# Second mixer of a hybrid trunk kernel: inverse kept in compact 32-column tiles, mean-free v, decays by ScalarE from running sums

## The reference

```python
r, k, v, xw, xa, xg = _split(h, RWKV_SPLITS)            # after the token shift mix
wlog = -softplus(-(w0 + tanh(xw) @ w2)) - 0.5
decay = exp(-exp(wlog))
a = sigmoid(a0 + xa @ a2);  g = sigmoid(xg) @ g2
kk = hd(k * k_k);  kk = kk / maximum(sqrt(sum(kk * kk)), 1e-12)
k = k * (1.0 + (a - 1.0) * k_a)
# scan over 512 tokens, 8 heads of 64:
sa = -einsum('bhvk,bhk->bhv', S, kk_t)
S = S * w_t + sa * (kk_t * a_t) + v_t * k_t;  y_t = S r_t
y = (y - mean(y)) * rsqrt(var(y) + eps)   # per head
y = (y * gn_g + gn_b + sum(r * k * r_k) * v) * g
# beside it, on the other 512 channels:
z = a_c * sigmoid(gate);  y_c = silu(layernorm(causal_conv31(z)))
```

## Time and profile before

| | |
|---|---|
| runs, median (lowest to highest) | 1389.52 us (1388.11 to 1390.04), 3 runs |
| profiled execution, own time | 1388.51 us |
| its span, mean granted clock | 1386.7 us, 0.967 |
| PE busy | 1279.2 us, 92%, 9060 instructions |
| PEld / DVE / ACT / POOL busy | 1038.0 / 682.2 / 421.6 / 518.6 us |
| w_hi*h_hi matmuls, L861, x696 | 283.7 us, 408 ns each |
| conv taps, L1807, x120 | 99.3 us, 827 ns each |
| w_lo, POOL, L501, x368 | 509.6 us, 1415 ns each |

### The profile page before, as it was taken

How to read it: one execution, slowest core, us unless ns; L and a number is a source line. 1 busy time by engine, 2 the same in 40 slices (tenths; PEclk the granted TensorE clock), 3 DMA queues, 4 the chain that set the end, 5 groups by cost and what they waited for, 6 DMA issues and landing times.

```text
span 1386.7 us, 21884 instructions
## 1 busy us (share of the span) xinstructions
PE 1279.2 (92%) x9060; PEld 1038.0 (75%) x9060; DVE 682.2 (49%) x992; ACT 421.6 (30%) x536; POOL 518.6 (37%) x374
## 2 busy tenths in 40 slices
PE   5999999999999999979798888787899999999997
PEld 4797978888888888856666656564688888888885
DVE  7435365551124444457758587675655511244334
ACT  4547333221122222253334324222432211222110
POOL 4341435554445555431121030110245544455541
PEclk9899999999999999989999999897999999999998
DMA  4331212222322223210011010000022232222221
GB/s 183 115 107 46 77 72 96 91 91 100 112 91 91 91 91 105 101 67 32 32 34 50 11 50 14 31 33 1 28 95 91 91 105 108 91 91 91 94 88 61
DMA packets 16808, 105.74 MB, mean 76 GB/s; under 512 B 1872, under 2 KB 2144, under 8 KB 4832
## 3 DMA queue, kind: packets, MB, share of 16 engines
q1 hardware_dynamic: 16304, 104.03, 21.1%
q10 hardware_dynamic: 432, 0.64, 0.1%
HBM read 102.57 MB, written 2.10 MB: 75 GB/s over the span
## 4 chain that ended last, share of the span: by engine, by line
issue 50%; PE 27%; POOL 21%; DVE 1%; DMA 0%; POOLq 0%; ACT 0%; SPq 0%; DVEq 0%
PE ps L861 23%; POOL w_lo L501 21%; PE ps L946 3%; PE ps L915 1%; DMA w_raw<-in_weights 0%; DVE x L1361 0%; PE ps L896 0%; POOL w_lo L490 0%; POOLq L495 0%; ACT w_hi L601 0%; POOLq L498 0%; SPq L454 0%; DVE xsq L1372 0%; DVE scaled L1431 0%; DVE x L1433 0%
## 5 line engine op out<-in xcount | busy, mean ns | idle before, releaser
L501 POOL TENSOR_TENSOR w_lo<-w_raw,w_hi 128x512 fp32r<-128x512 f32 x368 | 509.6, 1415 | 827.5 <-ACT w_hi L514 284.1
L861 PE MATMUL ps<-h_hi,w_hi 128*128 128x512 f32 x696 | 283.7, 408 | 11.6 <-POOL w_lo L490 11.6
L861 PE MATMUL ps<-h_lo,w_hi 128*128 128x512 f32 x696 | 275.0, 395 | 0.0
L861 PE MATMUL ps<-h_hi,w_lo 128*128 128x512 f32 x696 | 274.8, 395 | 0.0
L861 PEld LDWEIGHTS ps<-h_hi,w_hi 128*128 128x128 f32 x696 | 132.8, 191 | 51.3 <-issue 12.2
L589 ACT ACTIVATE w_hi<-w_raw 128x2048 fp32r<-128x2048 f32 x50 | 95.7, 1914 | 194.7 <-PE ps L861 143.4
L861 PEld LDWEIGHTS ps<-h_hi,w_lo 128*128 128x128 f32 x696 | 132.8, 191 | 28.7
L861 PEld LDWEIGHTS ps<-h_lo,w_hi 128*128 128x128 f32 x696 | 133.3, 192 | 25.9 <-issue 0.5
L861 PE MATMUL ps<-f_hi,w_lo 128*128 128x512 f32 x384 | 149.5, 389 | 0.0
L861 PE MATMUL ps<-f_hi,w_hi 128*128 128x512 f32 x384 | 149.5, 389 | 0.0
L861 PE MATMUL ps<-f_lo,w_hi 128*128 128x512 f32 x384 | 149.5, 389 | 0.0
(11 more groups left out here) (305 smaller groups left out, 1941.9 us busy)
## 6 DMA issues: line engine op xcount, KB each, us to landing
w_raw<-in_weights SPq DMA_DIRECT2D x93, 1024.0 KB, 4.9
outT<-x SPq DMA_DIRECT2D x8, 256.0 KB, 2.0
x<-in_xT SPq DMA_DIRECT2D x6, 256.0 KB, 7.3
masks_f<-in_masks SPq DMA_DIRECT2D x1, 768.0 KB, 10.6
x<-in_xT ACTq DMA_DIRECT2D x2, 256.0 KB, 5.6
w_raw<-in_weights SPq DMA_DIRECT2D x1, 512.0 KB, 6.4
low_w<-in_low_w SPq DMA_DIRECT2D x1, 512.0 KB, 11.3
sgu_ln<-in_sgu_ln SPq DMA_DIRECT2D x1, 512.0 KB, 3.6
```

The costliest lines, as they stand in the source:

```text
L501: piece = pool.tensor_tensor(w_lo[:, j, at], w_raw[:, j, at], w_hi[:, j, at].bitcast(f32), SUB)
L861: mm = pe.matmul(bank(gb(g) if isinstance(i, int) else g % 2), w, r, start=(k == 0 and m == 0), stop=(k == K - 1 and m == 2))
```

## The change

- **Inverse.** X and XT are block diagonal in 64 by 64 until the last level, so both are kept as `xc`, `xtc` (128 partitions, 8 matrices, 64 columns), as is TX (`txc`). `tx` and `dx` of levels 1 to 5 write 32 output columns each from 64 rows (`QUARTERS`), 32 columns moving: four matmuls per matrix for `tx`, four for the X update, and four for the XT update, which is now a step of its own, `dxt`, for all eight matrices at once (one VectorE copy instead of two). Level 6 makes only the off-diagonal quarter; ScalarE copies it into `XT`, and copies the two diagonals there (`xt_diag`). The banks alternate by level (`tx_bank`, `x_bank`).
- **Mean-free v.** v is brought to token rows by a matmul with `CEN` = identity - BLK/64 instead of a transpose, so that y comes out with no mean: the mean matmul, its subtraction and the step `yc` go. `ysq` is taken from the bank beside `y`. Gain and `gn_b` are folded into two VectorE steps; ScalarE's affine pass goes. `out_`, `conv_ln` and `taps` are split into single steps.
- **Decays.** The scan writes `cum`, with one zero column ahead of each chunk; ScalarE takes all exponentials from it, chunk by chunk, the chunk's middle as bias: 12 of 128 columns instead of 3 of 512, plus two scaled copies of 4 columns. Two VectorE subtractions go. `ak` moves from VectorE to ScalarE (`t_g`).
- **Order.** Slices are eighths (three matmuls), counts doubled. `evac_a`, `evac_q`, `evac_b` follow the last eighth of a tile at once, whatever comes next. `tok_tr` is a step of its own and waits for the X copies. `zpad` and `dsh` are double. A bank is free after `evac_a`. The tail is ordered anew.
- The mask table in DRAM shrinks from 1536 to 1025 columns.

The diff's core:

```diff
+QUARTERS = [(h, slice(a, a + 32)) for h in COLUMN_HALVES for a in (h.start, h.start + 32)]
...
             for lv in range(1, LEVELS):
-                ORDER1 += [("tx", c, lv, 0), ("tx", c, lv, 1)] + mid[lv] + fill(LEVEL_N[c][lv - 1])
-                ORDER1 += [("dx", c, lv, 0), ("dx", c, lv, 1)] + end[lv] + taps[lv]
+                ORDER1 += [("tx", c, lv, 0), ("tx", c, lv, 1)] + mid_[lv] + fill(LEVEL_N[c][lv - 1])
+                ORDER1 += [("xt_diag", c, 0), ("xt_diag", c, 1)] if lv == LEVELS - 1 else []
+                ORDER1 += [("dx", c, lv, 0), ("dx", c, lv, 1)]
+                if lv < LEVELS - 1:
+                    ORDER1 += [("dxt", c, lv)]
+                ORDER1 += end[lv] + taps[lv]
...
-            coming = [other[0] for other in ORDER1[at + 1:at + 4]]
-            if not scaled_yet or "dx" in coming:
+            if not scaled_yet:
                 continue
-            for t in begun:
-                order += [("evac_b", t), ("low", t)]
-            begun = []
             for t in held:
-                order += [("evac_a", t), ("evac_q", t)]
-                if t == held[-1] and t < 14 and coming[:1] in (["slice"], ["taps"]):
-                    begun += [t]
-                else:
-                    order += [("evac_b", t), ("low", t)]
+                order += [("evac_a", t), ("evac_q", t), ("evac_b", t)]
+                order += [("low", t)] if t < 2 else []
             held = []
...
+            def exps(c):
+                act.wait_ge(s("cum_done"), c + 1)
...
+                for dst, first, i, name, last in ((t_b, 0, 0, "ea_done", "at"), (t_c, 1, 1, "en_done", "kt"),
+                                                  (t_d, 1, 0, "ep_done", "rt")):
...
+                    for n in range(TT):
+                        one = act.activation(dst[:, n * P:n * P + P], cum[:, n, first:first + P], ACT.Exp,
+                                             bias=mid[:, i, n:n + 1], scale=(-EXP_HALF, EXP_HALF)[i])
...
+            def tok_tr(c, b):
+                pe.wait_ge(s("x_init"), 4 * c + 2)
...
+                    if b == 0:
+                        mm = pe.matmul(to, one, CEN[:, :], start=True, stop=True)
+                    else:
+                        mm = pe.transpose(to, one, IDENT)
...
                 for yy in range(4 * b, 4 * b + 4):
-                    for r in COLUMN_HALVES:
-                        mm = pe.matmul(as2(ps[r, 2 + b, 64 * (yy % 4):64 * (yy % 4) + 64], B), SC[:, yy, r],
-                                       half_of_one(X, yy, B, 0), start=True, stop=True)
+                    at = yy % 4
+                    if lv == LEVELS - 1:
+                        for to in (slice(64, 96), slice(96, 128)):
+                            mm = pe.matmul(ps[to, tx_bank(lv, b), 64 * at:64 * at + 64], SC[0:64, yy, to], xc[0:64, yy, :],
+                                           start=True, stop=True)
+                    else:
+                        for r, to in QUARTERS:
+                            mm = pe.matmul(as2(ps[to, tx_bank(lv, b), 32 * at:32 * at + 32], B), SC[r, yy, to],
+                                           side_of_one(xc, r, yy, B, 0), start=True, stop=True)
                 mm.then_inc(s("tx_mm"), 1)
...
+            def dxt(c, lv):
...
+                for yy in range(8):
+                    for r, to in QUARTERS:
+                        w = slice(to.start - r.start, to.stop - r.start)
+                        mm = pe.matmul(as2(ps[to, xt_bank(lv), 32 * yy:32 * yy + 32], B), txc[r, yy, w],
+                                       side_of_one(xtc, r, yy, B, 1), start=True, stop=True)
+                mm.then_inc(s("dxt_mm"), 1)
...
+            def xt_diag(c, h):
+                act.wait_ge(s("xt_upd"), 5 * c + 5)
...
+                r = COLUMN_HALVES[h]
+                act.activation(XT[r, :, r], xtc[r, :, :], ACT.Copy).then_inc(s("xt_diag"), 1)
```

More of the change, by code:

```diff
@@ L188, in build @@
             t_f = sb("t_f", [P, SEQ])
-            zpad = sb("zpad", [P, SEQ + TAPS - 1])
-            sgate = dsh
+            zpad = sb("zpad", [P, 2, SEQ + TAPS - 1])
             y = sb("y", [P, SEQ])
@@ L326, in build, with eighths @@
         TOK = {"v": (v_tok, 1), "sv": (sv, 5), "u": (u_tok, 7), "g": (g_tok, 9)}
-        def quarters(tiles):
-            return [("slice", t, q) for t in tiles for q in range(4)]
+        def eighths(tiles):
+            return [("slice", t, k) for t in tiles for k in range(KD)]
         def taps_in(c, counts):
             ends = [sum(counts[:i + 1]) for i in range(len(counts))]
[L336 to L341, removed]
-            + [("decay_v", 0, 2), ("kn", 0), ("kn_v", 0)] + quarters([14])[1:] + [("dyn", 0, 0)] \
-            + [("dyn", 0, 1)] + quarters([15])[:3] + [("bonus", 0), ("slice", 15, 3)]
+            return [[("tap", c, j) for j in range(e - n, e)] for n, e in zip(counts, ends)]
@@ new lines, in dyn @@
+        def dyn(c, names):
+            return [("dyn", c, name) for name in names]
+        ORDER1 = [("slice", t, k) for k in range(KD) for t in (0, 2)] + [("stat",)] \
+            + [("zero", i) for i in range(7)] + eighths([4]) + [("spread",)] + eighths([3])[:4] + [("zw", 0)] \
+            + eighths([3])[4:] + [("za", 0), ("ak", 0), ("scan", 0), ("ksq", 0), ("exps", 0)] \
+            + eighths([14])[:2] + [("ks", 0), ("ks_v", 0)] \
+            + [("dec", 0), ("kn", 0), ("kn_v", 0)] + eighths([14])[2:] + dyn(0, DYN[:3]) \
+            + dyn(0, DYN[3:]) + eighths([15])[:6] + [("bonus", 0)] + eighths([15])[6:]
@@ L351, in build @@
         for c in range(CT):
-            gaps = quarters(FILL[c])
+            gaps = eighths(FILL[c])
             def fill(n):
@@ L1827, in m @@
                 tt(M_LO1[k], M_SRC1[k], F(M_HI1[k]), SUB).then_inc(s("m_lo_done"), 1)
-            steps = {"stat": start, "spread": started, "evac_a": evac_a, "evac_b": evac_b, "decay_v": decay, "ks_v": ks, "kn_v": kn, "dyn": dyn, "bonus": bonus, "scores": scores,
-                     "dx": dx, "st": st, "post_v": post, "taps": taps, "conv_ln": conv_ln, "m": m}
+            steps = {"stat": lambda: norm(2), "zero": zero, "evac_a": evac_a, "evac_b": evac_b, "scan": scan, "dec": dec_,
+                     "ks_v": ks, "kn_v": kn, "dyn": dyn, "bonus": bonus, "scores": scores, "dx": dx, "dxt": dxt, "s": s_,
+                     "post_v": post, "tap": tap, "conv_sub": conv_sub, "conv_root": conv_root, "conv_scale": conv_scale, "m": m}
             for name, *a in ORDER1:
```

735 lines of the change are left out of this document (426 added, 309 removed).

## The result

The changed kernel is no faster: 1397.19 us, median of 15 runs (1388.41 to 1404.7), beside 1389.52 for the kernel before in as many. The ratio is 1.005, with a 95% interval of 1.0032 to 1.0068, so it is about 7 us slower, where 1370 was predicted with a range that ended at 1386. Runs 2 and 3 have one execution each in a slower state (1471.61 and 1499.3 us), which is left out of what is said of their time.

What follows compares the result with a forecast made beforehand. In the second mixer, TensorE with gaps bounds blocks 0 to 2, VectorE block 3. From 1388.5: -7.0 -8.9 -8.0 -5.5 -3.1 +2.5 +2.5 +1.0 +7.2 gives 1369.2, stated as 1370 us; range 1357 to 1386.

Steps and rivals of the forecast that it cites:

- The level matmuls: Levels 1 to 5 of the inverse: 192 records at 8 ns take 1.5 us a level, a gain of 1.3.
- the first step: Level matmul cadence, 1.5 us a level; wrong if a level's 192 records last over 2.5 us.
- Rival 3: tx, dx, dxt of levels 1 to 5: column tiles do not overlap, 29 ns a record, 1431 us; chance 0.06.
- The eager evacuations: Eager evac_b outside the first preparation leaves VectorE idle about 0.8 us a tile, mostly covered: 1.0 us slower.
- The first preparation: First block: `ak` and longer exponentials before the key norm's root, 1.6, and evac_b before dyn, 0.9: 2.5 us slower.
- Scores: v's real matmul with CEN and tok_tr waiting for the X copies: 2.5 us slower in sum.
- The clock: More TensorE idles of 3 to 4 us in blocks 0 to 2 lower the clock; four charged, 7.2 us.
- VectorE: VectorE's busy time falls by some 30 us through fewer copies, subtractions and updates.
- tail: Conv mean to output: mean matmul, its subtraction and ScalarE's affine pass leave the chain, 3.1 us gained.
- The sum of block 0: Block 0's six levels go from 43.0 to 36.0 us, 7.0 us gained.
- Second step's mark: TensorE's waits in 590 to 989 us: growth of more than 15 us would prove that step wrong.
- rival 2: Blocks 0 to 2: savings turn into waits through evacuations before copies and ScalarE's queue; 1384 us, chance 0.14.

Runs made afterwards that it cites:

- run 2: Changed kernel with level matmuls in 64 by 64 tiles, each issued twice: 1447.86 us, ratio 1.0449 to the kernel before.
- run 3: Kernel before with 1920 added small matmul records of 64 by 32 tiles in levels 1 to 5: 1482.31 us, ratio 1.0659.
- run 4: Changed kernel with dxt of levels 1 to 5 issued twice: 1433.98 us; with dxt for only four of eight matrices: 1380.59 us.
- run 1: Changed kernel with level matmuls in 64 by 64 tiles instead of 64 by 32: 1406.27 us, ratio 1.0098 to the kernel before.
- run 6: Old evacuation rule (none while dx is among the next three steps): on the changed kernel 1385.68 us, on its 64 by 64 form 1397.16 us.
- run 7: Changed kernel with block 0's twelve exponentials moved behind the key norm's square root on ScalarE: 1390.4 us.
- run 8: Changed kernel with old evacuation rule and block 0's exponentials behind the key norm's root: 1386.77 us; with tx also in 64 by 64 tiles: 1378.21 us.
- run 5: Changed kernel with only tx of levels 1 to 5 in 64 by 64 tiles: 1390.63 us.
- run 9: Unread wide matmuls in block 3 added to changed kernel 1398.53 us, to run 8's three-edit kernel 1377.59 us; kernel before with level matmuls over 64 rows 1396.27 us.

## Why the prediction was wrong

- **The level matmuls** (the step that failed). A level's 192 records took what I said while they ran: 8.6 ns each for 8, tx to tx 4.5 us in level 1 of block 0, as predicted. The sum took that cadence for the cost, and asked only how fast TensorE can start records, not how fast it gets them. Doubling the records doubled the instructions, and in this form each record costs 26 to 29 ns of time at the margin (run 4), nearly the 29 ns of the earlier trace rows. The gain of 1.3 us a level was paid back in waits for instructions, 25.7 us in the profile. By level stage they are 3.8, 4.2, 6.5 and 11.2 us; the stages of blocks 0 to 2 missed the forecast by 3.2, 5.4 and 9.0, and block 3's, meant to shrink, grew by 7.0. That 25.7 is also about what parts 1370 from 1397 is chance, since the misses below come on top. The record count stood in the text (544 to 1024 a block), and what it means for the instruction queue was nowhere. My test of the first step (192 records over 2.5 us) was aimed at the cadence: without a stall a level's records take 1.7 us; with one of 2.2 us, as in level 2 of block 0, they take 3.8, and the mark would have been passed.
- **Rival 3** had the right price, 29 ns a record, with the wrong mechanism (tiles that wait for each other), and its 1431 us counted on the 29 ns as TensorE's own work in every level. Runs 1 to 3 show that the mechanism exists in other forms: 27 to 28 ns for two 64 by 64 tiles in turn, 38 for mixed extents. The Trainium skill (TensorE: Matmul & The Clock Gate, "Wait — 56ns, not 53.3ns?") says that starts never come closer than about 25 ns; the trace does not agree for this form, whose records start 8.6 ns apart.
- **The eager evacuations**: charged at 1.0, and at longer levels 2 and 6 in block 0; run 6 measures 11.5. The place named for level 6 was right (waits before g name ScalarE's XT, 3.9 us at the longest, as said). The 0.9 charged to the first preparation does not show: it is as long with the old rule.
- **The first preparation**: exponentials and `ak` before the root, charged at 1.6; run 7 measures 6.8 alone, but nothing on top of the old rule (run 8). I set the exponentials at 2.2 to 3.2 us, and they took 3.6 behind a table load. From the first decay matmul to the spread of the key norm it is 17.9 us for 13.7, and 16.6 in four variants with the same preparation (runs 4, 5 and 9), so 3 to 4 us longer than before; run 7 has 12.1.
- **Scores**: charged at 2.5 for four blocks. From first score to first level matmul it is 17.7, 17.8, 18.8 and 22.1 us for 16.2, 16.1, 17.6 and 19.6: 6.9. The wait of tok_tr for the X copies (4.0 us in all) was in the text, and too small.
- **The clock**: charged at 7.2 for four idle stretches. The granted clock is 0.940 for 0.967 in the profiled runs, and 0.58 in all of block 3's levels. An estimate of what it costs takes the weight matmuls of 645 to 965 us, whose mean rose from 424 to 456 ns (three rows of 460, 406 and 406 before, of 497, 438 and 433 after, some 350 records), 11 us, and up to 4.6 us behind block 3, where the kernel before was not at full clock either. By this estimate the size was off by up to two; which stretches lowered the clock, and by what, is open (run 9). Over the 15 runs of the changed kernel the time falls with the clock, from 1404.7 us at 0.940 to 1388.4 at 0.954.
- **How the misses add up.** They sum to more than the 27 us between 1370 and 1397 (25 or so for the instructions, 10 for evacuations, 5 for the preparation, 4 for the scores, up to 8 for the clock). They overlap: the old rule and the exponentials behind the root alone share 8 us (run 8). How much of each run's gain is the clock's was not separated.
- **VectorE** was right, -30 us of busy time, and the **tail** in its direction: from conv variance to the end it is 5.4 us shorter (422.4 to 417.0), for 3.1 predicted.
- **The sum of block 0** has a slip: its six levels add to 36.15, not 36.0, which is 0.15 us and changes nothing.
- **Second step's mark**: waits in the mixer were to grow by more than 15 us if it was wrong. They grew by 17.4 (590 to 1000 us), and the waits for instructions, 25.7, are more than all of it. So rival 2 (savings turn into waits, 1384) is right in part: its own releasers, evacuations and ScalarE's queue, are there (runs 6 and 7), but the largest wait is one that it did not have.

## What to carry to other kernels

Short matmuls have two prices: the cadence that a burst shows, and two instructions each for which the supply asks 13 to 16 ns apiece once a stretch uses more than a block of them every 3 to 4 us. Before splitting matmuls into smaller tiles, count the instructions of a stretch against its length; when a wait of TensorE sits in the middle of a step and has no releaser, look at the instruction queue. Here the best mix was tiles of 32 columns for two steps of three and wider, slower ones for the third.

## What the hardware showed that was not expected

- TensorE stalled 18 times for 25.7 us in total, by up to 3.9 us, with all operands ready, while 16 KB instruction transfers came at best every 3.3 us; each stall ended 2.2 to 2.9 us after the start of one.
- In a burst, 64 by 32 tiles in four places start 8.6 ns apart; 64 by 64 tiles in two places 27 to 28 ns; tiles of 64 by 32 and 128 by 64 in turn 38 ns.
- With few and wide matmuls in its gaps TensorE's clock rose from 0.58 to 0.87 in block 3's levels and from 0.66 to 1.00 behind them; with the levels in 64 by 64 tiles of 32 moving columns it was 0.55, with each of these matmuls twice 1.00, and in 64 by 64 tiles of 64 moving columns 1.00.
